# Dummy matrix products ahead of TensorE's waits at the layer norms and the router

## What is computed

```python
for l in range(2):
    mix = hybrid_mixer(x, ...)                   # one input projection, pooling heads | mLSTM heads, output projection
    h = layer_norm(ALPHA * x + mix, ln1_g[l], ln1_b[l])
    if l == 0: f = swiglu(h, wg_dense, wu_dense, wd_dense)      # 1024 -> 2816 -> 1024
    else:      f = moe_swiglu(h, w_router, b_router, wg, wu, wd)  # top 2 of 8 experts, 1024 -> 3584 -> 1024
    x = layer_norm(ALPHA * h + f, ln2_g[l], ln2_b[l])
```

## Time and profile before

| | us |
|---|---|
| median of three runs | 1430.02 |
| the profiled execution, its own time | 1430.79 |
| its span, first to last instruction | 1428.8 |
| TensorE busy in it | 1317.5 (92%) |
| VectorE busy | 1142.5 (80%) |
| ScalarE busy | 938.6 (66%) |
| granted TensorE clock, mean | 0.974 |

### The profile page before, as it was taken

How to read it: one execution, slowest core, us unless ns; L and a number is a source line. 1 busy time by engine, 2 the same in 40 slices (tenths; PEclk the granted TensorE clock), 3 DMA queues, 4 the chain that set the end, 5 groups by cost and what they waited for, 6 DMA issues and landing times.

```text
span 1428.8 us, 18212 instructions
## 1 busy us (share of the span) xinstructions
PE 1317.5 (92%) x6740; PEld 1084.5 (76%) x6740; DVE 1142.5 (80%) x959; ACT 938.6 (66%) x743; POOL 124.2 (9%) x126
## 2 busy tenths in 40 slices
PE   7998999989998999988999998999998899999885
PEld 7898999979887788656788765678875577886663
DVE  6776554467576998898889789988879988988997
ACT  5543534445434776888777688867778886777885
POOL 3433000023522000000000000000000000000001
PEclk9999999999996999999999999999999999999998
DMA  9634555634435997998999799899899989979990
GB/s 330 221 122 167 176 196 186 193 130 166 159 118 192 347 355 289 399 409 334 387 409 374 282 409 398 317 404 402 294 366 391 391 319 410 388 275 398 409 358 31
DMA packets 133183, 425.12 MB, mean 298 GB/s; under 512 B 9280, under 2 KB 11616, under 8 KB 133104
## 3 DMA queue, kind: packets, MB, share of 16 engines
q1 hardware_dynamic: 131456, 419.17, 78.3%
q0 software_dynamic: 1504, 4.76, 1.1%
q10 hardware_dynamic: 144, 0.07, 0.0%
HBM read 422.92 MB, written 1.05 MB: 297 GB/s over the span
## 4 chain that ended last, share of the span: by engine, by line
PE 67%; DVE 15%; ACT 8%; issue 8%; DMA 1%; SPq 0%; ACTq 0%; DVEq 0%
PE bank L1456 17%; PE bank L1458 17%; PE bank L1457 17%; DVE w_lo L946 9%; ACT w_hi L667 6%; PE bank L1756 4%; PE bank L1757 4%; PE bank L1728 2%; PE bank L1752 2%; DVE arena L1018 1%; PE bank L1821 1%; DVE arena L1361 1%; DMA raw<-in_w_in 1%; ACT arena L852 1%; PE bank L1593 1%
## 5 line engine op out<-in xcount | busy, mean ns | idle before, releaser
L946 DVE TENSOR_TENSOR w_lo<-raw,w_hi 128x2048 fp32r<-128x2048 f32 x303 | 692.6, 2299 | 202.0 <-ACT w_hi L667 200.6
L667 ACT CAST w_hi<-raw 128x2048 fp32r<-128x2048 f32 x303 | 575.0, 1910 | 232.4 <-PE bank L1458 205.9
L1456 PE MATMUL bank<-w_hi,parts 128*128 128x512 f32 x824 | 332.0, 403 | 4.6 <-DVE w_lo L946 2.4
L1756 PE MATMUL bank<-w_hi,parts 128*128 128x512 f32 x672 | 281.6, 419 | 55.7 <-DVE w_lo L946 54.3
L1458 PE MATMUL bank<-w_hi,parts 128*128 128x512 f32 x824 | 322.1, 391 | 0.0
L1457 PE MATMUL bank<-w_lo,parts 128*128 128x512 f32 x824 | 321.8, 391 | 0.0
L1757 PE MATMUL bank<-w_lo,parts 128*128 128x512 f32 x672 | 264.5, 394 | 0.0
L1756 PEld LDWEIGHTS bank<-w_hi,parts 128*128 128x128 f32 x672 | 126.6, 188 | 121.2 <-DVE w_lo L946 86.9
L1456 PEld LDWEIGHTS bank<-w_hi,parts 128*128 128x128 f32 x824 | 155.2, 188 | 44.2 <-DVE w_lo L946 8.0
L1457 PEld LDWEIGHTS bank<-w_lo,parts 128*128 128x128 f32 x824 | 155.3, 188 | 33.1 <-issue 2.9
L1458 PEld LDWEIGHTS bank<-w_hi,parts 128*128 128x128 f32 x824 | 155.0, 188 | 33.3
(11 more groups left out here) (226 smaller groups left out, 1033.2 us busy)
## 6 DMA issues: line engine op xcount, KB each, us to landing
raw<-in_wg_exp SPq DMA_DIRECT2D x96, 1024.0 KB, 7.4
raw<-in_wd_exp SPq DMA_DIRECT2D x96, 1024.0 KB, 7.8
raw<-in_wu_exp SPq DMA_DIRECT2D x48, 1024.0 KB, 8.0
arena<-in_wu_exp SPq DMA_DIRECT2D x48, 1024.0 KB, 8.8
raw<-in_w_in SPq DMA_DIRECT2D x20, 1024.0 KB, 6.8
tokens<-in_wu_exp SPq DMA_DIRECT2D x16, 1024.0 KB, 8.1
raw<-in_wg_dense SPq DMA_DIRECT2D x11, 1024.0 KB, 5.1
raw<-in_wu_dense SPq DMA_DIRECT2D x11, 1024.0 KB, 5.1
```

What stands on the lines that cost most here:

```text
L667: a.copy(w_hi[:, n % SPLIT, :], slot(n)).then_inc(hi_ready, 1)
L946: v.tensor_tensor(w_lo[:, n % SPLIT, :], slot(n), w_hi[:, n % SPLIT, :].bitcast(F32), ALU.subtract).then_inc(lo_ready, 1)
L1456: mm(psum, left[0], right[0], start=first, stop=False)
L1756: mm(psum, left, right[0], start=first, stop=False)
```

## The change

A function `keep_busy(n, psum)` issues n products of a 128 x 128 block of `parts` with 512 columns of `parts`, each of which starts its sum anew in a PSUM bank that nobody reads before it is next overwritten. None of them waits or signals. They are put in front of waits that TensorE already has:

- in `turn` of norms 1 and 2: 10 before the wait for tile 0, 2 before the wait for tile 1;
- in `first_product` after norms 1 and 2: 7 before the wait for the rounded x;
- at the router: 5 between the turn of tile 0 and its first logits, 10 between the last logits and the wait for the chosen experts, 6 between the place counts and the gathers.

```diff
+            def keep_busy(n, psum):
+
+                for _ in range(n):
+                    mm(psum, parts[:, 0:P], parts[:, HALF:2 * HALF], start=True, stop=True)
+
             def turn(s, tiles=range(TT)):
                 for t in tiles:
                     if s == 0:
                         pe.wait_ge(x_in[t], 16)
                     else:
+                        if s < 3:
+                            keep_busy(10 if t == 0 else 2, bank[TURN_BANKS[t][0]])
                         pe.wait_ge(xhat_ready, TT * (s - 1) + t + 1)
...
             def first_product(psum, hi, lo, s):
 
+                if s:
+                    keep_busy(7, bank[0])
                 pe.wait_ge(xhi_ready, 2 * TT * s + TT)
...
             turn(3, [0])
+            keep_busy(5, bank[1])
             logits(0, range(0, 4))
             turn(3, [1])
             logits(0, range(4, DK))
             logits(1, range(DK)).then_inc(logit_mm, 1)
 
+            keep_busy(10, bank[4])
             pe.wait_ge(chosen_ready, 1)
             mm(bank[0][:, 2 * E:3 * E], tri, chosen[:, 0, :], start=True, stop=True)
             mm(bank[0][:, 3 * E:4 * E], ones, chosen[:, 0, :], start=True, stop=False)
             mm(bank[0][:, 3 * E:4 * E], tri, chosen[:, 1, :], start=False, stop=True).then_inc(pos_mm, 1)
+            keep_busy(6, bank[1])
```

## The result

The changed kernel takes 1442.84 us (median of 6 runs, 1441.42 to 1444.70), the kernel before beside it on the same chip 1430.07 (6 runs, 1429.59 to 1431.08): ratio 1.0089 [1.0076, 1.0102], so slower by 12.8 us where no change was forecast, and above the range. The profiled execution takes 1441.42 us with a span of 1439.4; before these were 1430.79 and 1428.8, so the two traces differ by 10.6 us of span.

The account below looks back on a forecast made before the run. The kernel was taken as mostly TensorE-bound (67% of the chain), the change touching only short waits. Norm 1 +0.3, norm 2 -0.3 and router -0.5 gave -0.5 us against 1430.79: 1430.3 us, range 1427.3 to 1434.0.

Parts of the forecast that it names:

- Does it pass on?: Item 0 to the end: TensorE is busy throughout, the ring full, so a shift of some us arrives unchanged.
- (4): Expert part: its transfers absorb any shift; 1430.0 us, chance 0.05.
- They stand before a wait that is already satisfied: Norm 1, ten dummies ahead of tile 0: they cover nothing and delay L677; cost 2.3 us, bounds 2.1 to 2.3.
- rival (1): Norms 1 and 2: the clock falls at both, in the gap before tile 1; +4.1 us, 1434.9; chance 0.15.
- What spoke against this rival: Expert-part waits up to 2.5 us leave the clock at 1.00; at the start, transposes alone had the clock raised.
- The return: Time regained if the clock holds: 2.0 us at norm 1, 2.6 at norm 2, bounds 0 and 2.6 at each.
- The new wait for L946 at the second dense unit: After norm 1: faster products then wait until 128.3 for the low part, so 2.0 of 2.6 us count.
- -0.3 was forecast: Norm 2, net: +2.3 us for the ten dummies less a return of 2.6 (0.5 + 2.1).
- -0.5 forecast: Router, net: -0.5 us, bounds -1.4 and +3.4, with the clock expected to drop somewhere in the logits.
- rival (3): Router: the clock is low when the ten and six dummies run; +3.4 - 0.5, 1433.7 us, chance 0.12.
- So its first products stay at low clock: Item 0: faster gathers only lengthen the idle gap before it, so its first products stay at low clock.
- The local one: Sum over norm 1, norm 2 and router: 0.3 - 0.3 - 0.5 = -0.5 us.

Follow-up runs that it names:

- the shift alone: The kernel before with 116 increments of an unused semaphore at TensorE's start and no dummy product: 1456.20 us beside 1430.75, ratio 1.0167.
- 16 increments: The changed kernel with 16 increments of an unused semaphore at TensorE's start, 250 instructions left in the loop's block: 1433.12 us, ratio 1.0019 to the kernel before.

## Why the prediction was wrong, step by step

**"Does it pass on?" failed.** It said that behind item 0 a shift arrives at the end unchanged. The shift that it had in mind did; but it took the expert part for the same program, because its source is, and so priced only what the new instructions do, not where they put those behind them. Item 0 to the end takes 989.14 us instead of 976.19: +12.95, against the -2.35 that item 0 brought. Of these 11.8 are the two jumps (shown by the shift alone, by 16 increments, and by the loop written out). The other 1.4 are item 0 itself, and that they come from the change is not shown: the kernel before with only its loop written out, the same program up to there, took 134.09 us for that piece instead of 132.47. No rival had it; (4), the only one about the expert part, was about transfers. The profile of before held a hint that I didn't follow: after a jump back the body's entry waits 2.55 and 2.53 us, where the first entry waits for nothing and no other wait of these products is over 1.70. These two are the longest of the earlier trace rows, which puts them down to L946 although its work was done. The Trainium skill, "Runtime: NRT & Kernel Launch", section "Instruction fetch mechanics", says that instruction memory is filled in blocks of 16 KiB, or 256 instructions, by a prefetch in order, and that a branch to a target outside the current two pages must have that page fetched before it goes on. The traces agree: the packets have 16,384 bytes, and at each jump back one starts and the body is entered some 2.7 us later (815.08 and 817.75 us in the changed kernel). That a second stop follows when few instructions of the block are left behind the target is shown by these runs: it came with 10 and with 26 left, and not with 50, 126, 250 and 254.

What is not settled: why the second fetch starts 5.6 to 6.5 us after the one before it, and what decides how long the clock is low behind an entry (0 to 6.8 us where no stop follows).

**Norm 1.** "They stand before a wait that is already satisfied" was right. Timelines of PE and ACT of the changed kernel:

```profile
114.56 0.39 PE L1458 MATMUL bank<-w_hi,parts 128*128 128x512 f32 x1
114.79 2.43 PE L1471 MATMUL bank<-parts 128*128 128x512 f32 x10
117.06 1.03 PE L1484 MATMUL bank<-cst,work 128*128 128x128 f32 x8
...
120.48 1.09 PE L1484 MATMUL bank<-cst,work 128*128 128x128 f32 x8 [1.92 <-DVE work L1154]
121.33 3.23 PE L1471 MATMUL bank<-parts 128*128 128x512 f32 x7
124.36 0.42 PE L1498 MATMUL bank<-x_hi,w_hi 128*128 128x256 f32 x1
...
119.08 0.30 ACT L677 ACTIVATE rstd<-mv,small 128x1 f32<-128x1 f32 x1
```

L677 starts 4.52 us after the last product instead of 2.25: 2.27 for a term of 2.1 to 2.3. That the clock holds was wrong here, so rival (1) came true at one of its two norms: it was low from 121.5 to 124.9, with two dummies in the gap ahead of tile 1. What spoke against this rival was also misread in part: behind the second of the two waits of 2.5 us in the earlier trace rows the clock fell, at 1059.6. The seven took 3.23 us instead of 1.6 and overran their gap, and the first product came 9.80 us after the last one of the mixer (9.0 forecast, 6.68 before). The return was mis-sized for it: 1.5 us instead of 2.0 (the piece from norm 1 to norm 2 is 193.46 us, less norm 2's ten 191.2, against 192.67). With ten in the gap it is 190.8, 1.9 less: the 2.0 was right for a clock that holds. The new wait for L946 at the second dense unit didn't show in the changed kernel, whose products came later by the low clock; with ten in the gap it is there, 0.46 us at 127.57.

**Norm 2.** The clock held in this trace, as it did with the loop written out; with 16 increments, and the same dummies, it fell here too (320.2, for 3.4 us), so at which norms rival (1) comes true differs between the runs. The return was mis-sized: 4.5 us instead of 2.6 (norm 2 to norm 3 takes 108.85 us, before 113.34), so the norm gave 2.2 us where -0.3 was forecast. Of the 4.5, 2.4 come behind the products that wait for the low parts (L1493), by the clock, where 2.1 were forecast. The other 2.1 come ahead of them, where 0.5 were forecast; they come from VectorE, and are told at the end.

**The router.** -0.5 forecast, -0.2 measured (24.04 us from norm 3 to item 0, before 24.23), by another road. Timeline of PE, and the row of VectorE that the ten should have ended with:

```profile
430.99 4.49 PE L1464 MATMUL bank<-rout_w,arena 128*128 128x8 f32 x24 [0.18 <-DVE arena L966]
435.34 4.20 PE L1471 MATMUL bank<-parts 128*128 128x512 f32 x10
439.38 0.28 PE L1731 MATMUL bank<-arena,cst 128*128 128x8 f32 x2
...
439.96 1.64 PE L1471 MATMUL bank<-parts 128*128 128x512 f32 x6
441.43 1.90 PE L1740 MATMUL bank<-parts,x_hi 128*128 128x128 f32 x16
...
450.26 0.77 PE L1456 MATMUL bank<-w_hi,parts 128*128 128x512 f32 x1 [5.14 <-issue]
```

```profile
437.80 0.17 DVE L1228 TENSOR_SCALAR arena<-arena 128x16 f32<-128x16 f32 x1
```

The ten ran at low clock, 4.20 us, and ended 1.4 us after `chosen` was there (437.97): part of rival (3). What they bought, gathers at high clock (1.90 and 1.95 us, 3.64), only made the gap before item 0 longer, 5.14 for 1.92 us, as said. In it the clock fell again (449.1, 6.8 us), and item 0 to the first scatter took 1.4 us more than in the one trace of the kernel before. "So its first products stay at low clock" was in the prediction; that they would stay there for longer was not.

**The sum.** The local one said -0.5 and the trace has -2.35 at item 0. Of this 0.7 us was there before the first dummy (the mixer's last product at 114.56 instead of 115.25), and the rest is +0.8 at norm 1, -2.2 at norm 2 and -0.2 at the router. With the +1.4 in item 0 itself, whatever its cause, it is -0.9 us: near the forecast, but by luck, since the terms were off by +0.5, -1.9 and +0.3 and offset each other. All the rest of the result, and its sign, is the one step that failed.

## What to carry to other kernels

Whoever adds or takes away instructions ahead of a hardware loop moves the loop in its 16 KiB block of code: look in the changed trace for waits for issue soon after each jump back, and, before blaming the edit, shift the loop by some instructions or write it out. Put work that only keeps an engine busy inside a gap that the profile shows, as long as the gap, and never ahead of a wait that is already satisfied: the same ten products cost 2.3 us there and nothing one tile later. The version with ten products in the gap, 20 ahead of item 0 and the loop written out takes 1419.86 us, 0.7% less than the kernel before.

## What the runs showed of the hardware that was not expected

With VectorE and GpSimd on large elementwise work side by side, the one that started second was slowed in these traces, and not the other. At norm 2, timelines of POOL and DVE of the kernel before, then of the changed one:

```profile
317.49 2.38 POOL L631 TENSOR_TENSOR tokens<-tokens,ln_row 128x1024 f32<-128x1024 f32 x1
317.95 4.27 DVE L973 TENSOR_TENSOR x_lo<-arena,x_hi 128x512 fp32r<-128x512 f32 x4
```

```profile
319.79 2.49 DVE L973 TENSOR_TENSOR x_lo<-arena,x_hi 128x512 fp32r<-128x512 f32 x4
319.86 4.68 POOL L631 TENSOR_TENSOR tokens<-tokens,ln_row 128x1024 f32<-128x1024 f32 x1
```

A shift of under 0.6 us between them changed which of the two took nearly twice as long. TensorE waits for L973 and not for L631, so its first product with the low parts came 2.1 us sooner in this order (9.46 us behind tile 0's turn, at 311.61, in the kernel before, and 7.39 in the changed one). No run was made for it alone.

An increment of a semaphore on TensorE costs 0.15 us at the start of the kernel: behind 76, 100 and 116 of them in a row the first transposes start at 12.6, 16.25 and 18.69 us. The 16 and 20 of other runs (some 3 us) lie beside the DMA that the first transposes wait for until 5.19.
